# Moving 32 modulation rows from the input projection into the attention of a two-block transformer kernel

## The reference, cut to what matters

```
mod = silu(c) @ w_mod + b_mod                  # c: one row of 1024; w_mod: 1024 x 6144
sh1, sc1, g1, sh2, sc2, g2 = split(mod, 6)
h   = rms_norm(x) * (1 + sc1) + sh1
q, k, v for two attentions = h @ w_in           # also for 256 context rows, with their own modulation
o_a = windowed attention with sink (8 heads, 2 kv heads)      # "a" heads
o_b = neighbourhood attention with bias table (8 heads)       # "b" heads
x   = x + g1 * (concat(norm(o_a), norm(o_b)) @ w_out)
h2  = rms_norm(x) * (1 + sc2) + sh2
x   = x + g2 * swiglu(h2)
```

## Time and profile before

| what | value |
|---|---|
| median of three runs | 2866.89 us |
| profiled execution, its own time | 2866.6 us |
| profiled execution, span from first to last instruction | 2864.8 us |
| PE busy | 2715.8 us (95% of the span) |
| PE weight loads busy | 2210.3 us (77%) |
| DVE busy | 1009.7 us (35%) |
| ACT busy | 964.3 us (34%) |
| POOL busy | 901.2 us (31%) |
| share of the last-ending chain | PE 85%, DVE 7%, issue 3%, ACT 3%, POOL 2%, DMA 1% |
| mean granted PE clock | 0.978 |

### The profile page before, as it was taken

One profiled execution on the slowest core, in us unless ns is written; L12 is line 12 of the kernel. 1 busy time (PEld: TensorE's weight loads), 2 busy tenths in 40 slices (PEclk: granted clock), 3 DMA queues, 4 the chain that ended last, 5 costly groups with the idle time before them and its releaser, 6 DMA issues.

```text
span 2864.8 us, 32292 instructions
## 1 busy us (share of the span) xinstructions
PE 2715.8 (95%) x13256; PEld 2210.3 (77%) x13256; DVE 1009.7 (35%) x1381; ACT 964.3 (34%) x1393; POOL 901.2 (31%) x452
## 2 busy tenths in 40 slices
PE   4799989999799999999999899999999999999996
PEld 3678769989777888888888577667768888888885
DVE  6653258878513212111121411123244223232323
ACT  2432457788523111111111442134143122222223
POOL 4211312355243323232324411112443233233234
PEclk7899999999999999999999999999999999999998
DMA  7242020122111121111111301000211111111112
GB/s 266 81 150 100 8 73 16 31 71 71 74 52 44 34 63 39 57 42 55 37 59 39 109 30 45 22 30 30 103 37 46 50 52 37 59 38 55 48 37 74
DMA packets 50708, 169.54 MB, mean 59 GB/s; under 512 B 6129, under 2 KB 6257, under 8 KB 50434
## 3 DMA queue, kind: packets, MB, share of 16 engines
q1 hardware_dynamic: 50562, 167.47, 18.5%
HBM read 148.31 MB, written 8.39 MB: 55 GB/s over the span
## 4 chain that ended last, share of the span: by engine, by line
PE 85%; DVE 7%; issue 3%; ACT 3%; POOL 2%; DMA 1%; SPq 0%; DVEq 0%; ACTq 0%; POOLq 0%
PE S L364 27%; PE S L365 27%; PE S L665 15%; PE S L567 2%; PE M L583 2%; DVE tt__105 L1405 2%; PE M L734 1%; PE S L551 1%; PE S L552 1%; PE M L367 1%; DVE mjk L1209 1%; PE S L749 1%; PE S L513 1%; DVE S L1367 1%; PE S L521 1%
## 5 line engine op out<-in xcount | busy, mean ns | idle before, releaser
L1585 POOL TENSOR_TENSOR wl<-raw,wh 128x1024 fp32r<-128x1024 f32 (+2 forms) x227 | 469.0, 2066 | 1421.9 <-ACT wh L801 1421.9
L801 ACT ACTIVATE wh<-raw 128x1024 fp32r<-128x1024 f32 (+2 forms) x227 | 209.7, 924 | 1330.1 <-PE S L365 886.3
L364 PE MATMUL S<-hh,wh 128*128 128x512 f32 (+1 forms) x1176 | 479.4, 408 | 62.0 <-DVE hcl L1239 27.7
L364 PE MATMUL S<-hl,wh 128*128 128x512 f32 (+1 forms) x1176 | 460.4, 392 | 4.8 <-POOL hl L1697 3.4
L365 PE MATMUL S<-hh,wh 128*128 128x512 f32 (+1 forms) x1176 | 461.7, 393 | 0.0
L364 PE MATMUL S<-hh,wl 128*128 128x512 f32 (+1 forms) x1176 | 461.3, 392 | 0.0
L365 PE MATMUL S<-hh,wl 128*128 128x512 f32 (+1 forms) x1176 | 461.0, 392 | 0.0
L365 PE MATMUL S<-hl,wh 128*128 128x512 f32 (+1 forms) x1176 | 460.4, 392 | 0.0
L364 PEld LDWEIGHTS S<-hh,wh 128*128 128x128 f32 (+1 forms) x1176 | 221.8, 189 | 123.9 <-issue 67.3
L364 PEld LDWEIGHTS S<-hl,wh 128*128 128x128 f32 (+1 forms) x1176 | 221.0, 188 | 58.5 <-POOL hl L1697 8.1
L364 PEld LDWEIGHTS S<-hh,wl 128*128 128x128 f32 (+1 forms) x1176 | 221.5, 188 | 48.6 <-issue 0.6
(11 more groups left out here) (270 smaller groups left out, 3703.3 us busy)
## 6 DMA issues: line engine op xcount, KB each, us to landing
mr<-in_w_modT SPq DMA_DIRECT2D x32, 512.0 KB, 4.8
raw<-in_w_d SPq DMA_DIRECT2D x48, 256.0 KB, 2.6
raw<-in_w_f1g SPq DMA_DIRECT2D x22, 512.0 KB, 3.5
raw<-in_w_f1u SPq DMA_DIRECT2D x22, 512.0 KB, 3.4
raw<-in_w_f2g SPq DMA_DIRECT2D x22, 512.0 KB, 3.5
raw<-in_w_f2u SPq DMA_DIRECT2D x22, 512.0 KB, 3.5
raw<-in_w_d SPq DMA_DIRECT2D x32, 320.0 KB, 2.9
raw<-in_w_in SPq DMA_DIRECT2D x18, 512.0 KB, 3.5
```

What stands on the lines that cost most here:

```text
L364: e.matmul(S[j][0:mm, 0:512], lhs, x[:, k, 0:512], start=first, stop=last)
L801: e.activation(flat(wh[:, w % 2, :, :])[:, 0:n], raw[:, (w + NPM) % 3, 0:n], ACT.Copy).then_inc(*w_hi.mark(w))
L1585: e.tensor_tensor(l, raw[:, (w + NPM) % 3, 0:n], h.bitcast(F), ALU.subtract).then_inc(*w_lo.mark(w))
```

## The change

The 32 rows leave the input projection and go into the attention. Rows 0 to 13 are computed in items 0 to 55: POOL multiplies the row by `cb` (in iterations with i % 4 == 1) and ACT sums it with an accumulating Copy (i % 4 == 3). Rows 14 to 31 stay with DVE's `tensor_tensor_reduce`, in two halves of 512 columns each, one half in every odd iteration from 57 to 127. The Silu of `cb` goes behind the last unit of the projection, ahead of ACT's preparation of heads 0 and 1. The buffers change places: `bt` lies over the raw slabs, `cb` and `mr` over the converted ones. So SP loads the first three slabs of the output projection only after the last use of `bt`, and the first conversion of an output slab waits for row 31. SP's loads of `cb`, of the first tables and of the first three rows wait for DVE's last scaling in the projection.

```
@@ buffers
-    bt = at("bt", A_W, [128, 2, 1472], F)
-    cb = at("cb", P_QA, [128, 1024], F)
-    mr = at("mr", P_QA + 4 * KB, [128, 3, 1024], F)
+    bt = at("bt", A_RAW, [128, 2, 1472], F)
+    cb = at("cb", A_W, [128, 1024], F)
+    mr = at("mr", A_W + 4 * KB, [128, 3, 1024], F)
@@ scalar_program
                 if w == FIRST["out"]:
-                    e.wait_ge(*d_nm(NI - 1))
+                    e.wait_ge(*d_mr(31))
...
             split_hi(2)
-            e.wait_ge(*l_cb(0))
-            e.activation(cb[:, :], cb[:, :], ACT.Silu).then_inc(*a_set.mark("cb"))
             split_hi(3)
...
             unit_norm(NU - 1)
+            e.wait_ge(*l_cb(0))
+            e.activation(cb[:, :], cb[:, :], ACT.Silu).then_inc(*a_set.mark("cb"))
             e.wait_ge(*l_sink(0))
...
             e.wait_ge(*p_rope(13))
-            e.wait_ge(*d_nrm(NU - 1))
...
                     e.activation(ot[:, i % 2, :], M[i % 2][:, 0:256], ACT.Copy).then_inc(*a_ot.mark(i - 2))
+                if i % 4 == 3 and i < 56:
+                    n = i // 4
+                    r = mr[:, n % 3, :]
+                    e.wait_ge(*p_mr(n))
+                    e.activation(r, r, ACT.Copy, accum_out=mv[:, M_RAW + 16 + n:M_RAW + 17 + n]).then_inc(*a_mod.mark(n))
@@ vector_program
-                if u == 10:
-                    e.wait_ge(*d_mr(31))
...
-            def mod_rows(s):
-                for n in range(4 * s - 4, 4 * s):
-                    r, c = mr[:, n % 3, :], M_RAW + 16 + n
-                    e.wait_ge(*l_mr(n))
-                    if n == 0:
-                        e.wait_ge(*a_set("cb"))
-                    else:
-                        e.wait_ge(*d_mr(n - 1))
-                    e.tensor_tensor_reduce(r, r, cb[:, :], 1.0, 0.0, ALU.mult, ALU.add, mv[:, c:c + 1]).then_inc(*d_mr.mark(n))
...
                         e.tensor_tensor(lo, src, hi.bitcast(F), ALU.subtract).then_inc(*d_pl.mark((i - 1, half)))
+                if i >= 56 and i % 2 and i < 128:
+                    n, half = i // 4, i // 2 % 2
+                    r, c = HALF[half], mv[:, M_RAW + 16 + n:M_RAW + 17 + n]
+                    e.wait_ge(*l_mr(n))
+                    ...
+                    e.tensor_tensor_reduce(mr[:, n % 3, r], mr[:, n % 3, r], cb[:, r], 1.0, c if half else 0.0, ALU.mult, ALU.add,
+                                           c).then_inc(*d_mr.mark(n if half else (n, 0)))
@@ the sums with b_mod and norm2_g move from the projection's end to the attention's end
@@ gpsimd_program
+                if i % 4 == 1 and i < 56:
+                    n = i // 4
+                    r = mr[:, n % 3, :]
+                    e.wait_ge(*l_mr(n))
+                    if n == 0:
+                        e.wait_ge(*a_set("cb"))
+                    e.tensor_tensor(r, r, cb[:, :], ALU.mult).then_inc(*p_mr.mark(n))
@@ sync_program
-                if s == 11:
-                    ...
-                    e.dma_start(cb[:, :], T["c_row"].to_broadcast([128, 1024])).then_inc(*l_cb.inc(0))
-                while n < min(32, 3 + 4 * (s - 11)):
-                    load_mr(n)
-                    n += 1
-            e.wait_ge(*made(NU - 1))
+            e.wait_ge(*d_ev(NU - 1))
+            e.wait_ge(*d_nrm(NU - 1))
+            e.dma_start(cb[:, :], T["c_row"].to_broadcast([128, 1024])).then_inc(*l_cb.inc(0))
             e.dma_start(snk[:, 0:8], T["sink"].to_broadcast([128, 8])).then_inc(*l_sink.inc(0))
             for h in range(2):
                 e.dma_start(bt[:, h, :], T["bias"][h]).then_inc(*l_bias.inc(h))
+            def load_mr(n):
+                if n >= 32:
+                    return
+                if n >= 3:
+                    e.wait_ge(*(a_mod if n - 3 < 14 else d_mr)(n - 3))
+                e.dma_start(mr[:, n % 3, :], T["w_modT"][16 - NPM + n]).then_inc(*l_mr.inc(n))
+            for n in range(3):
+                load_mr(n)
...
-            for w in range(FIRST["out"], FIRST["out"] + 3):
-                load_slab(NPM + w, w_lo(w - 3))
...
+                if i % 4 == 3:
+                    load_mr(i // 4 + 3)
+            load_slab(NPM + FIRST["out"], d_nm(NI - 1))
+            for w in range(FIRST["out"] + 1, FIRST["out"] + 3):
+                load_slab(NPM + w)
```

More of the change, by code:

```diff
@@ L332, in build @@
         a_vv, a_k, a_exp, a_pt, a_ot, a_bt = (signal("a_" + n) for n in ("vv", "k", "exp", "pt", "ot", "bt"))
-        a_sink, a_osq, a_hh, a_act = (signal("a_" + n) for n in ("sink", "osq", "hh", "act"))
+        a_mod, a_sink, a_osq, a_hh, a_act = (signal("a_" + n) for n in ("mod", "sink", "osq", "hh", "act"))
         a_gate, a_gd, a_v, a_q, a_o, a_gsq = (signal("a_" + n) for n in ("gate", "gd", "v", "q", "o", "gsq"))
@@ L341, in build @@
         d_gn, d_tap, d_fin = signal("d_gn"), signal("d_tap"), signal("d_fin")
-        p_xr, p_hl, p_rope, p_k, p_v = (signal("p_" + n) for n in ("xr", "hl", "rope", "k", "v"))
+        p_xr, p_hl, p_rope, p_k, p_v, p_mr = (signal("p_" + n) for n in ("xr", "hl", "rope", "k", "v", "mr"))
         p_out, p_osc, p_x2, p_fl, p_gsq, p_fin = (signal("p_" + n) for n in ("out", "osc", "x2", "fl", "gsq", "fin"))
@@ L1299, in vector_program @@
             unit_norm(0)
-            mod_rows(1)
             for s in range(2, NU):
@@ L1305, in vector_program @@
                 unit_take(s)
-                if s <= 8:
-                    mod_rows(s)
             unit_norm(NU - 1)
-            e.tensor_tensor(mv[:, M_MOD + 16:M_MOD + 48], mv[:, M_RAW + 16:M_RAW + 48], vec[:, V_BMOD + 16:V_BMOD + 48],
-                            ALU.add).then_inc(*d_mv.mark("mod"))
-            e.wait_ge(*d_mv("mod"))
-            e.scalar_tensor_tensor(mv[:, M_G2:M_G2 + 8], mv[:, M_MOD + 32:M_MOD + 40], 1.0, vec[:, V_N2:V_N2 + 8],
-                                   ALU.add, ALU.mult).then_inc(*d_mv.mark("g2"))
             e.wait_ge(*p_rope(13))
@@ L1378, in vector_program @@
                         e.tensor_tensor(lo, src, hi.bitcast(F), ALU.subtract).then_inc(*d_pl.mark((i - 1, half)))
+                if i >= 56 and i % 2 and i < 128:
+                    n, half = i // 4, i // 2 % 2
+                    r, c = HALF[half], mv[:, M_RAW + 16 + n:M_RAW + 17 + n]
+                    e.wait_ge(*l_mr(n))
+                    if i == 57:
+                        e.wait_ge(*a_set("cb"))
+                    elif half:
+                        e.wait_ge(*d_mr((n, 0)))
+                    else:
+                        e.wait_ge(*d_mr(n - 1))
+                    e.tensor_tensor_reduce(mr[:, n % 3, r], mr[:, n % 3, r], cb[:, r], 1.0, c if half else 0.0, ALU.mult, ALU.add,
+                                           c).then_inc(*d_mr.mark(n if half else (n, 0)))
+            e.wait_ge(*d_mr(31))
+            e.tensor_tensor(mv[:, M_MOD + 16:M_MOD + 48], mv[:, M_RAW + 16:M_RAW + 48], vec[:, V_BMOD + 16:V_BMOD + 48],
+                            ALU.add).then_inc(*d_mv.mark("mod"))
+            e.wait_ge(*d_mv("mod"))
+            e.scalar_tensor_tensor(mv[:, M_G2:M_G2 + 8], mv[:, M_MOD + 32:M_MOD + 40], 1.0, vec[:, V_N2:V_N2 + 8],
+                                   ALU.add, ALU.mult).then_inc(*d_mv.mark("g2"))
             def turn_out(k):
```

8 lines of the change are left out of this document (removed).

## The result

The changed kernel took 2891.8 us (median of four runs, 2889.22 to 2894.3), the kernel before 2866.74 beside it. The ratio is 1.0086, with a 95% interval of 1.0072 to 1.01. The forecast was 2891.5.

A forecast was written before the change was run, and what follows sets the result against it. PE was taken to bound the projection, with all engines close to full in the attention. −5.9 + 1.5 + 4.2 + 21.1 + 4 = +24.9 on 2866.6 gave 2891.5 us; own range 2882 to 2904, whole range 2872 to 2907.

The forecast's parts named there:

- projection: End of unit 1: without ACT's wait for `cb`, PE's wait shrinks to 2.3 us and clock time comes back; −5.9 us.
- the attention's beginning, head 0 with it: Before PE's first scores: later conversion of queries and DMAs queued behind tables and rows; 0.4 to 3.5 us, taken as +1.5.
- rows 0 to 13: Items 0 to 55: POOL's products cost nothing, ACT's sums delay PE about 0.3 us a row; +4.2 us, between nothing and 8.
- the halves' own time, × 0.9: Heads 7 to 15 at b1, b3, b5: 0.84 us halves exceed 0.41 idle; 11.6 us, nine tenths reaching PE, +10.4.
- POOL blocking, × 0.9, and the clock: Heads 7 to 14: halves at b1 wait for POOL's subtraction, 11.9 us × 0.9; clock falls behind PE's waits, +4.
- D: Attention's beginning: the 3.0 MB queued ahead is served in full and the clock falls, +5 instead of +1.5; 2895, within the forecast's 0.55.
- A: Attention: the moved work fits into idle time and only the projection's gain and the beginning count; −4.4, 2862 us; chance 0.10.
- B: Attention: DVE and POOL don't block each other, halves cost only their own time; +10.2, 2877 us; chance 0.15.
- C: Attention: every POOL operation blocks, casts and TENSOR_SCALAR too, and the clock falls in all five heads; 2899.5 us; chance 0.15.

The follow-up runs named there:

- e7: The kernel before, with only the Silu of `cb` moved behind the norm of unit 0 and nothing moved into the attention: 2862.54 us, ratio 0.9984.
- e1: The changed kernel with DVE's halves at b3, b5, b6 and b7 of heads 7 to 15 instead of b1, b3, b5 and b7: 2876.74 us.
- e2: The changed kernel with each half row at its old place but with one input, a plain sum without the product with `cb`: 2869.76 us.
- e8: The kernel of e3 with three more two-column DVE additions, all in SBUF, in each iteration from 57 to 127: 2907.85 us, a single run.
- e4: The changed kernel with SP's loads of `cb`, tables and first rows asked for earlier, and the Silu behind the copies of the values: 2886.84 us.
- e11: The changed kernel with only SP's loads asked for earlier, the Silu staying ahead of the first queries: 2885.24 us, ratio 1.0064.
- e6: The changed kernel with ACT's sum of rows 0 to 13 over 2 columns only, POOL's products kept: 2889.26 us, ratio 1.0078.
- e9: The changed kernel with one-input halves without the product with `cb`, placed at b3, b5, b6 and b7: 2872.45 us, ratio 1.0019.
- e3: The changed kernel with each two-input half row over 2 columns instead of 512: 2880.77 us, ratio 1.0048.

## Why the prediction was right in its sum, and where its terms were wrong

The direction, the collisions with POOL and the late beginning came as forecast. That the total is 0.3 us from the median is luck: two terms were too small by 4.6 and some 6 us, two too large by 1.7 and over 9, and the changed kernel's own runs lie 5 us apart.

| term | predicted | in the trace |
|---|---|---|
| projection | −5.9 | −5.8 |
| the attention's beginning, head 0 with it | +1.5 | +6.1 |
| rows 0 to 13 | +4.2 | +2.5 |
| the halves' own time, × 0.9 | +10.4 | +0.6 to +1.3 |
| POOL blocking, × 0.9, and the clock | +14.7 | +20.1 to +20.8 |
| sum | +24.9 | +24.2 |

*The projection* went as its step says. The end of unit 17 came at 360.31 in place of 366.14 us. The wait shrank to 2.46 us, predicted 2.3. The clock stayed at 1.00 in the changed kernel and in e7; in e1, e2 and e8 it was at 0.50 for one stretch of 3.4 us behind the same wait of 2.46. So this part of the gain is not certain in each execution.

*The beginning* is the term that was mis-sized. Its mechanism was named, with 0.4 to 3.5 us for PE's wait, and it measured 3.25. D had 3 us for the data ahead in the queue, the trace has 3.9. I took 1.5 for it, where D, all of it served first, came close. The other part was the clock: 6.8 us at 0.50 behind the wait, so that item 1 took 4.87 us instead of 2.58. e4 and e11 take the wait away, and the half clock and 5 to 6.6 us of the time go with it. D's +5 was near.

*Rows 0 to 13.* Net 0.19 us a row instead of 0.3. The bound from below was nothing, and the row on which it rested (0.47 us of idle time) is of b4 in one head; the forecast took no account of what the next item gives back. That it is the sum and not the product is shown by e6.

*The halves' own time* is the second mis-sized term, and here the step itself failed. I had reasoned that a half displaces DVE's 0.41 us of idle time and that nine tenths of the rest reach PE. Both figures were in the rows, but the nine tenths came from one delay of 0.92 us at b0, and I laid them on a remainder of 0.43. With one input (e2) the half takes 0.68 us at all 36 places and nine heads are 0.6 us longer in all. With two inputs head 15 of the changed kernel, whose halves meet nothing of POOL, is 0.14 longer, which makes 1.3 for nine. A delay that DVE makes good before the next item's inputs are there reaches nobody. It holds for halves in every second item: with three in four items a head is 0.27 longer (e9).

*POOL and the clock* cost more than the forecast had, and take up what was missing. The six waits at b1 were as long as worked out (2.94 against 2.5 + 0.68 in head 7, 1.85, 2.7 four times), and at b1 of heads 9 and 14 there was none of this kind, where 0 and 0.4 us had been forecast. Two more I had not laid out: L1640, POOL's subtraction for the queries, which begins when the half does at b7 of heads 8 and 13, because both follow the same scores. I had taken the b7 as covered by the wait for the bias table, but 2.9 us aren't covered by 1.03. The clock was at 0.50 for 3.4 us at five waits of 2.1 to 2.3 us, in heads 7, 10, 11, 12 and 14, and not behind those at 587.08 [2.29], 603.52 [2.23] and 700.22 [2.12]. Head 13 had the same collision at b1 as heads 10 to 12 and full clock: 25.08 us against 26.53 to 26.93. So a fall cost 1.5 to 1.9 us (the forecast's 1.7), and five of them, less the one of head 9 that the kernel before had the earlier trace rows and the changed one hadn't, about 7 us instead of 4. The rest, about 13, is the collisions, where the forecast had 10.7.

*The rivals.* A (2862) fell: PE stands behind the half rows. But its reason was half right: the idle time is enough for work that isn't held by POOL (e2). B (2877, no blocking) fell with the first long row, and with e1, e2 and e3. C (2899.5, every POOL operation blocks) had the mechanism right and the price wrong. Casts do hold a half, as e8 shows, but the halves of the changed kernel met next to none: 0.11 us at b7 of head 7, 0.04 at b1 of head 9, where I had 0.6. And L1682, the L1673 of before, holds for its first 0.7 us only; for it I had 0.9 at b3 of four heads, and it came to lie beside b7 instead (DVE, then POOL, head 9):

```profile
608.81 0.74 DVE L1373 CUSTOM_DVE_ANT_0 mr<-mr,cb,mv 128x512 f32<-128x512 f32 x1
...
607.52 1.57 POOL L1682 TENSOR_SCALAR oa<-oa,ors 128x512 f32<-128x512 f32 x1
```

The half begins 1.29 us into it and takes its usual 0.74. By the Trainium skill, GPSIMD Engine Reference, section 1 (Specifications), the contention is with VectorE instructions that have two SBUF inputs, and it sets no kind of GpSimd operation apart. The runs agree on both, with 2.7 us against 0.68 beside the same L1645 (e2), and 0.88 against 0.15 beside a cast (e8); for the TENSOR_SCALAR they agree for its first 0.7 us. My forecast, that only subtractions block, was the wrong one of the two and lost nothing by it here.

D had the attention's beginning right: the data served first, the clock falling in the wait, +5 where +6.1 was measured. Its total, 2895, is 3 us too high, because the other terms were off too.

## What to carry to other kernels

Before work is moved to DVE, ask of it two things: has it two inputs in SBUF, and what does POOL run at that moment. A two-input operation that begins within a subtraction or cast of POOL waits for what that has left, however small it is itself, and with 512 columns of its own it holds POOL's next one in turn; a one-input operation of the same size can be nearly free even where PE is busy for 22.1 of 23 us, and so can a two-input one at the right place. And ask first whether the gain needs the move: here all of it was one wait in ACT's order, and moving one instruction behind the next norm brought nearly all of it alone (e7), while the loads that moved along cost as much again (6.1 us against 5.8).
